# A two-block diffusion trunk on one core: parameters and first unit loaded in parts, weight conversions and half of the output product moved into the two attention stages

## What is computed

```python
def trunk_layer(xl, xc, ml, mc, norm_w, ...):          # twice
    xl = xl + 0.5 * g1l * swiglu(modulate(rmsnorm(xl, norm_w[0]), sh1l, sc1l), w_ffn1_in, w_ffn1_out)
    xc = xc + 0.5 * g1c * swiglu(...)                  # the same on the context
    mix_l, mix_c = token_mixer(hl, hc, w_in, ...)      # low-rank attention of 8 heads joined to a gated short convolution
    xl = xl + g2l * mix_l
    xl = xl + 0.5 * g3l * swiglu(modulate(rmsnorm(xl, norm_w[2]), sh3l, sc3l), w_ffn2_in, w_ffn2_out)
    ...
def second_block(x, ...):                              # once: mLSTM and HGRN mixer, then a convolved FFN
    xl = xl + g1 * (concatenate([ml_l, hg_l]) @ w_out)
    xl = xl + g2 * conv_ffn(modulate(rmsnorm(xl, norm2_w), sh2, sc2))
```

## Time and profile before

| | us |
|---|---|
| median of 3 runs | 2159.15 (2157.16 to 2160.31) |
| the profiled execution | 2158.99 |
| its span in the profile | 2157.2 |
| PE busy in the span | 2099.9 |
| mean granted TensorE clock | 0.992 of full speed |

### The profile page before, as it was taken

One profiled execution on the slowest core, in us unless ns is written; L12 is line 12 of the kernel. 1 busy time (PEld: TensorE's weight loads), 2 busy tenths in 40 slices (PEclk: granted clock), 3 DMA queues, 4 the chain that ended last, 5 costly groups with the idle time before them and its releaser, 6 DMA issues.

```text
span 2157.2 us, 28636 instructions
## 1 busy us (share of the span) xinstructions
PE 2099.9 (97%) x11118; PEld 1754.0 (81%) x11118; DVE 1505.3 (70%) x2642; ACT 920.4 (43%) x1525; POOL 231.7 (11%) x149
## 2 busy tenths in 40 slices
PE   7999999999999999999999999989999999999998
PEld 5788888885788888888888888958888788979987
DVE  3777778665578776557567555768866587778995
ACT  4422222435553222225232223556565454656553
POOL 1000000006000000000000000030000000017861
PEclk9999999999999999999999999999999999999999
DMA  7455555331135555543555554415655433124544
GB/s 290 171 193 194 194 195 205 117 112 55 40 118 185 193 192 194 203 156 137 176 184 196 194 190 154 137 60 180 230 189 185 144 106 103 48 79 146 187 164 149
DMA packets 61846, 342.08 MB, mean 159 GB/s; under 512 B 6672, under 2 KB 8720, under 8 KB 32144
## 3 DMA queue, kind: packets, MB, share of 16 engines
q1 hardware_dynamic: 60528, 338.56, 45.2%
q10 hardware_dynamic: 1184, 1.70, 0.3%
HBM read 339.19 MB, written 1.05 MB: 158 GB/s over the span
## 4 chain that ended last, share of the span: by engine, by line
PE 85%; DVE 10%; ACT 2%; issue 1%; DMA 1%; POOL 0%; SPq 0%; DVEq 0%; ACTq 0%; POOLq 0%
PE bank L621 39%; PE bank L629 20%; PE bank L641 7%; DVE arena L2703 5%; PE bank L649 4%; PE bank L754 2%; PE bank L1034 2%; PE bank L763 1%; ACT w_hi L1300 1%; DVE w_lo L1891 1%; PE bank L671 1%; PE bank L1055 1%; PE bank L1043 1%; PE bank L1136 1%; DMA raw<-stream 1%
## 5 line engine op out<-in xcount | busy, mean ns | idle before, releaser
L1300 ACT ACTIVATE w_hi<-raw 128x1024 fp32r<-128x1024 f32 (+1 forms) x429 | 445.5, 1038 | 978.0 <-PE bank L621 875.2
L1891 DVE TENSOR_TENSOR w_lo<-raw,w_hi 128x1024 fp32r<-128x1024 f32 (+1 forms) x379 | 453.6, 1197 | 424.1 <-ACT w_hi L1300 419.1
L621 PE MATMUL bank<-h_hi,w_hi 128*128 128x512 f32 (+1 forms) x1288 | 428.7, 348 | 1.8 <-DVE h_lo L2389 1.3
L621 PE MATMUL bank<-h_lo,w_hi 128*128 128x512 f32 (+1 forms) x1288 | 426.4, 346 | 0.0
L621 PE MATMUL bank<-hidden_hi,w_hi 128*128 128x512 f32 x1024 | 399.2, 390 | 1.0 <-DVE squares L2123 1.0
L621 PE MATMUL bank<-hidden_lo,w_hi 128*128 128x512 f32 x1024 | 398.9, 390 | 0.0
L1924 DVE CUSTOM_DVE_ANT_0 scratch<-columns_raw,late,params 128x1024 f32<-128x1024 f32 x288 | 359.9, 1278 | 7.7 <-issue 7.4
L621 PEld LDWEIGHTS bank<-h_hi,w_hi 128*128 128x128 f32 x1288 | 243.8, 189 | 33.2 <-DVE h_lo L2389 1.6
L621 PEld LDWEIGHTS bank<-h_lo,w_hi 128*128 128x128 f32 x1288 | 243.9, 189 | 30.2 <-issue 0.5
L629 PE MATMUL bank<-h_hi,w_lo 128*128 128x512 f32 (+1 forms) x1288 | 266.0, 347 | 0.6 <-POOL w_lo L2812 0.5
L629 PE MATMUL bank<-hidden_hi,w_lo 128*128 128x512 f32 x1024 | 254.5, 390 | 3.4 <-DVE w_lo L1891 3.4
(11 more groups left out here) (332 smaller groups left out, 2397.8 us busy)
## 6 DMA issues: line engine op xcount, KB each, us to landing
raw<-stream SPq DMA_DIRECT2D x221, 1024.0 KB, 5.0
columns_raw<-columns_in SPq DMA_DIRECT2D x176, 512.0 KB, 3.7
arena<-sides_in SPq DMA_DIRECT2D x6, 1024.0 KB, 10.8
x<-x_in SPq DMA_DIRECT2D x4, 512.0 KB, 16.1
late<-cond_in SPq DMA_DIRECT2D x2, 1024.0 KB, 4.9
columns_raw<-sides_in SPq DMA_DIRECT2D x1, 1024.0 KB, 22.3
late<-sides_in SPq DMA_DIRECT2D x1, 1024.0 KB, 23.6
x<-ctx_in ACTq DMA_DIRECT2D x1, 1024.0 KB, 5.7
```

What stands on the lines that cost most here:

```text
L621: last = nc.tensor.matmul(acc, w_hi[:, buffer, kc, :], v(first_chunk + kc), start=start and kc == n == 0, stop=False)
L1300: nc.scalar.activation(w_hi[:, buffer, 0:chunks, :], raw[at % RING][:, 0:chunks, sub * P:(sub + 1) * P], ACT.Copy)\
L1891: nc.vector.tensor_tensor(w_lo[:, buffer, 0:chunks, :], raw[at % RING][:, 0:chunks, sub * P:(sub + 1) * P], w_hi[:, buffer, 0:chunks, :].b ...
```

## The change

1. **Loads.** The parameters are laid out anew: the first 112 columns (`HEAD_PARAMS`) hold what the start needs and are loaded first, the rest after x. `sum_rows` becomes the first 32 columns of the constants and is loaded alone. Unit 0 is loaded in two halves of 128 columns (pieces of 512 bytes), the first ahead of x and the second behind it, followed by the other constants and parameters.
2. **Conversions at the start.** `convert(fourth, 0)` comes ahead of `finish_silu(0)` and `finish_unit(0)`; `cond_silu(0)` moves from step 4 to step 1 of the first FFN on ACT.
3. **Beginning of both attention stages.** The converts of `out{i}, 0` leave the place ahead of the loop: ACT makes them in steps 4 and 6, DVE in steps 5 and 7. A dummy exponential ahead of ACT's head steps loads the table early. PE's scores wait for value 0 only, the first turn of probabilities for the rest. In the second layer `rope(1)` comes after the last key step.
4. **End of both stages.** The chunks of the convolution's rows (4 to 7) of both halves of `out{i}, 0` are multiplied inside the loop's end and right behind it (`out_high`, `out_low`); the chunks 0 to 3 follow once `attended` is complete. The convolution's steps are each up to three steps earlier.

The "second mixer" code is the same in both kernels.

```diff
 PARAMS, N_PARAMS = _columns(
-    [(f"norm{i}", 3 * KC) for i in range(DEPTH)] + [(f"b_ada{i}", N_MOD * KC) for i in range(DEPTH)]
+    [("c1", 2 * KC), ("norm0", 3 * KC), ("b_ada0", N_MOD * KC), ("norm1", 3 * KC), ("b_ada1", N_MOD * KC)]
...
+HEAD_PARAMS = (2 + 3 + N_MOD) * KC
...
-        CONV_STEPS = [[len(attention_units(t)) * (c + 1) // 4 - 1 for c in range(4)] for t in (0, CTX)]
+        CONV_STEPS = [[len(attention_units(t)) * (c + 1) // 4 - 1 - c for c in range(4)] for t in (0, CTX)]
+        OUT_HIGH, OUT_LOW = (4, 6), (5, 7)
...
-            sp.dma_start(params[:, :], params_in).then_inc(sem("params_loaded"), 16)
+            sp.dma_start(params[:, 0:HEAD_PARAMS], params_in[:, 0:HEAD_PARAMS]).then_inc(sem("params_loaded"), 16)
             for j in range(SCALE_UNITS):
                 sp.dma_start(side_raw[j], sides_in[j]).then_inc(side_full[j], 16)
-            sp.dma_start(consts[:, 0:EARLY_CONSTS], consts_in[:, 0:EARLY_CONSTS]).then_inc(loaded, 16)
+            sp.dma_start(consts[:, 0:32], consts_in[:, 0:32]).then_inc(sem("sum_rows_loaded"), 16)
...
-                sp.dma_start(raw[n % RING][:, :, :], stream[n]).then_inc(unit_full[n % RING], 16)
                 if n == AT["up10", 0]:
+                    sp.dma_start(raw[0][:, :, 0:P], stream[0][:, :, 0:P]).then_inc(sem("first_half"), 16)
                     for j in range(X_PARTS):
                         some = slice(j * KC // X_PARTS, (j + 1) * KC // X_PARTS)
                         sp.dma_start(x[:, some, :], x_in[:, some, :]).then_inc(x_full[j], 16)
+                    sp.dma_start(raw[0][:, :, P:], stream[0][:, :, P:]).then_inc(unit_full[0], 16)
+                    sp.dma_start(consts[:, 32:EARLY_CONSTS], consts_in[:, 32:EARLY_CONSTS]).then_inc(loaded, 16)
+                    sp.dma_start(params[:, HEAD_PARAMS:], params_in[:, HEAD_PARAMS:]).then_inc(sem("later_params"), 16)
+                else:
+                    sp.dma_start(raw[n % RING][:, :, :], stream[n]).then_inc(unit_full[n % RING], 16)
...
+            def out_high(sub, t0, chunks, start=False):
+
+                half, marks = At.half + sub, []
+                pe.wait_ge(half_high, half + 1)
+                for kc in chunks:
+                    for v in (h_hi,) if t0 else (h_hi, h_lo):
+                        marks.append(nc.tensor.matmul(bank[OUT_BANK[sub]][:, :], w_hi[:, half % 2, kc, :], v[:, kc, :],
+                                                      start=start and not marks, stop=False, skip_group_check=True))
+                return marks
+
+            def out_low(sub, t0, chunks, stop=False):
+
+                half = At.half + sub
+                pe.wait_ge(half_ready, half + 1)
+                for kc in chunks:
+                    last = nc.tensor.matmul(bank[OUT_BANK[sub]][:, t0:], w_lo[:, half % 2, kc, :], h_hi[:, kc, t0:], start=False,
+                                            stop=stop and kc == chunks[-1], skip_group_check=True)
+                return last
+
             def out_product(name, update, t0, norm_after, await_chunk=None):
                 for j in range(4):
                     full_wait(pe, AT[name, j])
+                    if j == 0 and not await_chunk:
+                        for sub in range(2):
+                            begun = out_high(sub, t0, range(KC // 2))[0]
+                            if sub == 1:
+                                begun.then_inc(half_begun, 1)
+                            out_low(sub, t0, range(KC // 2), True).then_inc(sem("acc_ready"), 1)
+                        At.half += 2
+                        continue
...
-                pe.wait_ge(sem(f"query_moved{tag}"), head_moves(len(HEAD_STEPS), t0 == 0))
+                pe.wait_ge(sem(f"query_moved{tag}"), head_moves(HEAD_STEPS.index(("value", 0)) + 1, t0 == 0))
...
                         pe.wait_ge(sem("exp"), seen(i) + m + 1)
+                        if m == 0:
+                            pe.wait_ge(sem(f"query_moved{tag}"), head_moves(len(HEAD_STEPS), t0 == 0))
...
+                            if m == c == 0:
+                                last.then_inc(half_begun, 1)
                         last.then_inc(sem("prob_turned"), 1)
+                    if n == len(units):
+                        pe.wait_ge(sem("conv_out"), 4 * i + 4)
+                        out_high(1, t0, range(KC // 2, KC), True)[1].then_inc(unit_begun, 1)
...
+                out_high(0, t0, range(KC // 2, KC), True)
+                for sub in range(2):
+                    out_low(sub, t0, range(KC // 2, KC))
                 pe.wait_ge(sem("attended"), seen(i) // 2 + len(units) // 2)
-                pe.wait_ge(sem("conv_out"), 4 * i + 4)
                 out_product(f"out{i}", tag, t0, f"norm3{i}")
...
-            pe.wait_ge(loaded, 16)
+            pe.wait_ge(sem("sum_rows_loaded"), 16)
             side_turn(0)
...
                 buffer = At.half % 2
-                full_wait(act, at)
+                if At.half:
+                    full_wait(act, at)
+                else:
+                    act.wait_ge(sem("first_half"), 16)
...
+                convert(fourth, 0)
                 finish_silu(0)
-                convert(fourth, 0)
...
                         high(p - 1, p - 1)
+                        if norm_name == "norm10" and p == 1:
+                            cond_silu(0)
                         continue
...
-                    if (name, p) in (("10", 4), ("11", COND_STEP)):
-                        cond_silu(int(name == "11"))
+                    if (name, p) == ("11", COND_STEP):
+                        cond_silu(1)
...
-                    if n < 7 and (n or name != "out"):
+                    if 0 < n < 7:
                         convert(AT[name, (n + 1) // 2], (n + 1) % 2)
...
+                nc.scalar.activation(small[:, 72:73], const("eps"), ACT.Exp)
                 for n, (what, j) in enumerate(HEAD_STEPS):
...
-                convert(AT[f"out{i}", 0], 0)
                 if i == DEPTH - 1 and until is None:
...
+                    if n in OUT_HIGH:
+                        convert(AT[f"out{i}", 0], OUT_HIGH.index(n))
...
+                if n == 0:
+                    dve.wait_ge(sem("later_params"), 16)
                 dve.wait_ge(column_full[n % COLUMN_RING], 16 * (n // COLUMN_RING + 1))
...
                 bias_to_rows(0)
+                convert(fourth, 0)
                 finish_unit(0)
-                convert(fourth, 0)
...
-                        if j == 1:
+                        if j == (HEADS // 2 - 1 if t0 else 1):
                             rope(1)
-                convert(AT[f"out{i}", 0], 0)
...
+                    if n in OUT_LOW:
+                        convert(AT[f"out{i}", 0], OUT_LOW.index(n))
```

12 lines of the change are left out of this document (8 added, 4 removed).

## The result

The changed kernel took **2143.27 us** (median of six runs, 2142.78 to 2144.35), the kernel before 2159.67 in the runs beside it: a ratio of 0.9928 with a 95% interval of 0.9919 to 0.9938. The profiled execution took 2142.99 us with a span of 2141.2, 16.0 us under the span before. Forecast were 18.4 us less and 2140.6: direction and range held, and the forecast is 2.7 us too low.

What follows compares the result with a forecast made beforehand. PE, busy 97% of the span, was taken as the bound, so only its idle gaps counted. The terms 1.5 - 0.2 + 5.0 + 3.2 + 2.1 + 5.6 + 1.2 = 18.4 us took 2158.99 to 2140.6, range 2135.5 to 2147.0.

Steps and rivals of the forecast that it cites:

- the first attention: Begin of the first layer's attention: 2.5 us before the first turn plus 1.3 of clock, less 0.6 for converts: 3.2 won.
- The failed step: First attention's loop: the converts moved inside cost 0.6 us, between bounds of nothing and 4.6, as scores run two units ahead.
- rival (a): Attention loops: converts cost half of 4.6 us per stage, 4 us more than counted, 2144.6; chance 0.18.
- The first loads: Start of the kernel: with the new load order, DVE's low parts, which pace PE, begin 1.5 us earlier.
- The silu: Conditions' silu in the first FFN: done earlier on ACT, it removes PE's wait for `w_lo` and slow matmuls, 5.0 us won.
- rival (b): First FFN: the early silu does not free DVE in time, PE still waits near 82 us; 3 us worse, 2143.6; chance 0.12.
- The convert swap: Start, before unit 3 of the first FFN: ACT's convert ahead of the table load delays unit 0's gate, 0.2 us lost.
- Second begin: Begin of the second attention: key copies no longer wait for `rope(1)`, the first turn comes at 1418.2, 5.6 us won.
- The ends: Ends of both attention stages: convolution-row products fill PE's gaps, 2.1 us won in the first and 1.2 in the second.
- (c): Whole kernel: more goes than counted, small waits and a clock staying high, 2 to 4 us, 2137.5; chance 0.13.
- (d): First loads: 512-byte pieces take a fixed time each, x comes late, 18 us slower, 2177; chance 0.02.
- (e): Both attention stages: the early exponential's table is displaced and loaded again, 1.3 us in each, 2143.2; chance 0.03.

Runs made afterwards that it cites:

- silu table: Changed kernel with ScalarE's function table for the silu called up by a one-element silu directly behind the first norm's square root; 2140.51 us.
- late low converts: Changed kernel with only VectorE's two low converts of the first layer's attention moved from steps 5 and 7 to 21 and 23; 2141.54 us.

## Why the prediction was right, and where it was not

- **Direction and range** held because the gain is a sum of idle gaps of an engine that is busy 98%, and each gap was read from its own rows. Six of seven terms came within 0.4 us. Of the 2.4 us missing in the span, 1.6 are the first attention (converts 2.0 dearer, clock 0.4 better) and 0.6 the tail of the same code.
- **The failed step:** "I take 0.6, nearer to the lower end", for the converts inside the first attention's loop. They and the convolution's new steps cost 2.6 us, 2.2 of it seen as waits. The reason given (scores run two units ahead) leaves out that every unit also needs DVE's row maximum, in DVE's order: a low convert that makes the row maximum 1.2 us late delays the exponential, ACT's own convert then stands ahead of the copy, and the turn waits. The window in the earlier trace rows was taken at 540 us, behind the end of POOL's convolution, and shows neither stretched converts nor the place in a head pair where DVE has no room. That is rival (a), half of the converts' length, true in the first layer and false in the second, where no wait appeared.
- **A part without a price:** the convolution's steps. "POOL ended it long before" answers whether the data is there, not what DVE's operation displaces; a wait of 0.45 us, 0.6 by the starts.
- **The first loads** came out by their arithmetic (1.5 forecast, 1.68 at DVE), partly by luck, since the medians over all profiles differ by 1.1. The end of the chain was set by PE's clock, which the sum left out: 1.18. No row of before could show it, since there the clock rose in time.
- **The silu:** 4.7 of 5.0; PE waits 0.24 us at 77.44 behind the displaced silus, so rival (b) was there in small, without the fall of the clock. The convert swap cost nothing that shows.
- **Second begin:** 5.2 of 5.6; right against the profiled execution, but 1.7 us of it were that execution's clock, so that the number fits is in part luck. The tail of the same code gave 0.6 us the other way; over the profiles it spreads from 693.8 to 696.3.
- **The ends:** 2.3 of 2.1 and 1.5 of 1.2. Sixteen matmuls in 3.80 us are 0.24 each, not 0.227; that moves the term by 0.3 us at most.
- **Rivals (c), (d), (e)** did not come. The table of the exponential was loaded in ACT's idle time in both layers and no load stands ahead of the first true one.

What stays open: which execution sees the clock fall behind a wait, and for how long, and how much the stretch beside POOL adds to what the low converts' place costs. The fall was seen in the changed loop in two of its variants (behind the same two waits of 1.08 and 0.61 us: clock 0.51 from 518 to 521 us with the silu table, 0.6 us lost) and not in the two others that have these waits.

## What to carry to other kernels

Work put into a loop "where the engine has idle time" has to be placed by step, not by share: read which operation stands behind it in the queue, who waits for that one, and which other engine's work stretches it there. Where gaps of a saturated engine are added up, price the clock behind each gap separately and look for it in more than one execution. And before calling a moved step free because its data is ready, ask what it now stands in front of.

## What was not expected of the hardware

- DVE operations with SBUF operands alone took up to 1.38 us instead of 0.29 beside POOL's convolution (a row of the kernel with late low converts, and one of the kernel before), and POOL's own 2.13 and 2.60 us instead of 1.27 and 1.56; those reading PSUM did not change.
- The clock behind the same wait of 2.25 us fell in one execution (ten matmuls in 5.40 us) and stayed in two (3.71).
- The first transfers alone move the start of the work by up to 1.5 us from one execution to another (17.85 to 19.36 us with the same loads).
